# A two-layer diffusion / flow-matching step on one core: grid tokens by columns, norms in two halves, the last tiles of a stage in halves

## The reference

```python
def _modulate(x, mod, s, g):
    h = _rms_norm(x, g)
    return h * (1 + mod[:, :, 3 * s + 1]) + mod[:, :, 3 * s]
def _ffn_sublayer(x, mod, s, g, w13, w2):
    return x + 0.5 * mod[:, :, 3 * s + 2] * _swiglu(_modulate(x, mod, s, g), w13, w2)
```

## Time and profile before

| | |
|---|---|
| median of three runs | 3238.27 us |
| the profiled execution's own time | 3244.05 us |
| its span, first to last instruction | 3242.2 us |
| busy TensorE matmul / weight load | 3171.7 / 2917.7 us |
| busy VectorE / ScalarE / GpSimd | 1477.7 / 905.4 / 287.6 us |
| mean granted TensorE clock | 0.989 of full speed |
| moved by DMA | 300.25 MB, 93 GB/s |

### The profile page before, as it was taken

One profiled execution on the slowest core, in us unless ns is written; L12 is line 12 of the kernel. 1 busy time (PEld: TensorE's weight loads), 2 busy tenths in 40 slices (PEclk: granted clock), 3 DMA queues, 4 the chain that ended last, 5 costly groups with the idle time before them and its releaser, 6 DMA issues.

```text
span 3242.2 us, 48789 instructions
## 1 busy us (share of the span) xinstructions
PE 3171.7 (98%) x19680; PEld 2917.7 (90%) x19680; DVE 1477.7 (46%) x2313; ACT 905.4 (28%) x1279; POOL 287.6 (9%) x366
## 2 busy tenths in 40 slices
PE   8899999999999999999999999999999999999999
PEld 4899999976979999999999999868697876999999
DVE  3565634247654665624652525253443524422323
ACT  4122214234454312224212124222212222421222
POOL 1000001012001000001000001030301104000001
PEclk9999999989999999999999999999999999999999
DMA  8443422221101444422442222212121211122222
GB/s 210 151 170 132 156 78 65 86 70 25 61 1 53 149 163 136 162 82 75 160 152 75 102 69 84 84 59 72 65 72 65 79 68 36 65 78 78 72 72 72
DMA packets 84911, 300.25 MB, mean 93 GB/s; under 512 B 10399, under 2 KB 12735, under 8 KB 84000
## 3 DMA queue, kind: packets, MB, share of 16 engines
q1 hardware_dynamic: 57888, 206.77, 18.5%
q0 software_dynamic: 20704, 74.89, 8.1%
q10 hardware_dynamic: 6176, 16.54, 1.4%
HBM read 290.67 MB, written 8.44 MB: 92 GB/s over the span
## 4 chain that ended last, share of the span: by engine, by line
PE 90%; DVE 3%; ACT 2%; DMA 2%; issue 2%; POOL 1%; SPq 0%; ACTq 0%; DVEq 0%; POOLq 0%
PE ps L1227 36%; PE ps L1212 30%; PE ps L1366 11%; PE ps L1422 2%; PE ps L1588 2%; PE ps L1397 2%; PE ps L1597 2%; ACT tmp_g L507 1%; DMA ada<-in_ada 1%; PE ps L1410 1%; PE ps L1576 1%; DMA x<-in_xT 1%; PE ps L1243 1%; PE ps L1248 1%; DVE negmax L991 0%
## 5 line engine op out<-in xcount | busy, mean ns | idle before, releaser
L1227 PE MATMUL ps<-h,w 128*128 128x320 f32 x8640 | 1278.7, 310 | 19.1 <-DVE w L799 18.7
L1227 PEld LDWEIGHTS ps<-h,w 128*128 128x128 f32 x8640 | 1271.1, 188 | 25.1 <-DVE w L799 20.0
L1212 PE MATMUL ps<-g,w 128*128 128x320 f32 x5376 | 793.1, 309 | 1.5 <-DVE g L1173 1.5
L1212 PEld LDWEIGHTS ps<-g,w 128*128 128x128 f32 x5376 | 790.5, 188 | 2.2 <-issue 2.2
L799 DVE TENSOR_TENSOR w<-raw,w 128x1024 fp32r<-128x1024 f32 x383 | 460.8, 1224 | 288.6 <-ACT w L482 282.8
L482 ACT ACTIVATE w<-raw 128x1024 fp32r<-128x1024 f32 x207 | 216.3, 1060 | 562.6 <-PE ps L1212 457.9
L1366 PE MATMUL ps<-w,h 128*128 128x512 f32 x1596 | 368.5, 391 | 3.1 <-ACT rv L741 3.1
L1366 PEld LDWEIGHTS ps<-w,h 128*128 128x128 f32 x1596 | 298.0, 188 | 67.0 <-issue 4.7
L898 DVE TENSOR_TENSOR tmp_g<-tmp_s,ps 128x640 f32<-128x640 f32 x88 | 72.3, 821 | 598.3 <-ACT tmp_s L523 598.3
L819 DVE CUSTOM_DVE_ANT_0 prod<-ada,crow 128x1024 f32<-128x1024 f32 x256 | 298.5, 1219 | 17.5 <-DMA ada<-in_ada 17.4
L523 ACT ACTIVATE tmp_s<-ps 128x640 f32<-128x640 f32 x88 | 62.0, 705 | 846.2 <-PE ps L1227 846.2
(11 more groups left out here) (161 smaller groups left out, 1854.2 us busy)
## 6 DMA issues: line engine op xcount, KB each, us to landing
raw<-in_ws SPq DMA_DIRECT2D x383, 512.0 KB, 3.6
ada<-in_ada POOLq DMA_DIRECT2D x132, 512.0 KB, 3.9
ada<-in_ada ACTq DMA_DIRECT2D x6, 1024.0 KB, 16.9
rst<-in_state ACTq DMA_DIRECT2D x4, 1024.0 KB, 4.7
out_new_state<-rsx ACTq DMA_DIRECT2D x8, 512.0 KB, 2.7
bias<-rp_rep POOLq DMA_DIRECT2D x16, 224.0 KB, 4.3
x<-in_xT SPq DMA_DIRECT2D x1, 2560.0 KB, 25.6
crow<-in_crow POOLq DMA_DIRECT2D x1, 1024.0 KB, 6.0
```

The lines of the kernel that those rows point to most:

```text
L1212: mm = pe.matmul(pair_half(pr, half, width), w2[:, slot, wi, at:at + cols], rhs(k, ri)[:, half * width:(half + 1) * width], start=(k == 0 ...
L1227: mm = pe.matmul(pair_half(pr, half), w2[:, n % RING, wi, k * P:(k + 1) * P], h2[:, k, ri, half * HT:(half + 1) * HT], start=(k == 0 and w ...
```

## The change

**Tokens by grid columns.** The latents enter column by column (the host reorders them), and x goes back to grid rows in the first output projection of the attention (`add_by_rows`, which reads with a stride of 8 tokens); the query of the latent attention is reordered likewise (`latent_hi`, `latent_lo`, the rope). A block of 128 queries is then 16 grid columns, whose keys lie in a window of 192 or 256 latents (`NA_WINDOW`). Scores, maximum, exponential, normalisation run over 320 or 384 columns instead of 640, with 3 transposes and 3 value pieces in place of 5. V is made in 6 token tiles at window offsets (`V_AT`) in place of 5. The host lays out the bias rows, so `rp_rep` is gone; a head has one contiguous DMA of 128 KB and three GpSimd adds (640 columns in all). Two dummy matmuls of 512 columns (`dense`) stand in each unit, and the first score, the first exponential and the evacuation of V now overlap the V projection.

**Halves.** The last 4 tiles of an FFN (6 of the two projections ahead of norms 2 and 5) run twice: all for tokens 0 to 319, then all for 320 to 639. The first half's norm runs beside the second half's tiles; the broadcast, the sums and the h chunks are per half (16 half chunks in place of 8). The next stage's first two tiles are done by halves too. A chunk is now scale-and-multiply (VectorE), shift-and-split (ScalarE, one step instead of two), low part (VectorE). Weight splits of the next stage are moved ahead of or between the chunks, and `keep_warm` remains only at the start. The conditioning rows `crow` are loaded and passed through SiLU a second time before FFN 1, because the attention's buffers now cover them.

```diff
+MH = [5, 4, 2, 4, 4, 2, 4]
...
+            def half_lines(nn, h, l, s, after):
+                xn = x_cols if nn < 2 else x
+                dve.wait_ge(n_rb, 2 * nn + h + 1)
+                for k in range(KD + 2):
+                    if k < KD:
+                        if k >= 4:
+                            dve.wait_ge(h_lo, chunk(nn, h, k - 4))
+                        for c0, c1, st in half_parts(h):
+                            ins = dve.scalar_tensor_tensor(tmp_u[:, k % 4, c0:c1], xn[:, k, c0:c1], amul[:, k, st:st + 1],
+                                                           pair(2)[:, c0:c1], ALU.mult, ALU.mult)
+                        ins.then_inc(n_u, 1)
+                    if k >= 2:
+                        dve.wait_ge(h_hi, chunk(nn, h, k - 2))
+                        for c0, c1, st in half_parts(h):
+                            ins = dve.scalar_tensor_tensor(h2[:, k - 2, 1, c0:c1], tmp_u[:, (k - 2) % 4, c0:c1],
+                                                           mod[:, NMOD * l + 3 * s, k - 2, st:st + 1],
+                                                           h2[:, k - 2, 0, c0:c1].bitcast(fp32), ALU.add, ALU.subtract)
+                        ins.then_inc(h_lo, 1)
+                    if k in after:
+                        after[k]()
...
+            def norm_tail(nn, add1, lines, blocks):
+                add1(MH[nn])
+                if nn in PROJ:
+                    add1(MH[nn] + 1)
+                half_var(nn, 0)
+                if len(blocks) > 1:
+                    blocks[0]()
+                half_diag(nn, 0)
+                for m in range(MH[nn] + (2 if nn in PROJ else 1), KD - 2):
+                    add1(m)
+                lines(0, {1: blocks[1] if len(blocks) > 1 else lambda: None, 2: lambda: add1(KD - 2),
+                          3: lambda: add1(KD - 1), 6: lambda: half_var(nn, 1), 7: lambda: half_diag(nn, 1)})
+                lines(1, {3: blocks[-1]})
...
+                    for h in range(2):
+                        for m in range(mh, KD):
+                            n = rb + 2 * nf + m
+                            if h == 0:
+                                have(n)
+                            half_free(NORM_AFTER[q], xb + 8 * r, m, h)
+                            half_tile(n % RING, m % 3, of_g, h, nf).then_inc(wt_free if h else dn_half, 1)
+                            if h and m == mh:
+                                half_sum(NORM_AFTER[q], 0)
+                            elif h and m == mh + 1:
+                                half_rb(NORM_AFTER[q], 0)
...
+            def halves(ns, prs, nn):
+                for h in range(2):
+                    for k in range(KD):
+                        if nn and h == 0 and k == 4:
+                            half_sum(nn, 1)
+                        if nn and h == 0 and k == KD - 1:
+                            half_rb(nn, 1)
+                        pe.wait_ge(h_lo, chunk(nn, h, k))
+                        for n, pr in zip(ns, prs):
+                            for wi, ri in ((0, 0), (0, 1), (1, 0)):
+                                mm = pe.matmul(pair_half(pr, h), w2[:, n % RING, wi, k * P:(k + 1) * P],
...
 attend:
                 for g in range(g0, g1):
                     if g + 2 < g1:
                         score_mm(g + 2, na)
+                    if na:
+                        dense(1)
                     weight_mm(g, na)
+                    if na:
+                        dense(1)
                     if g - 1 >= g0:
                         value_mm(g - 1, na)
...
-            pool.dma_start(a["rp_rep"].rearrange("r (e w) -> r e w", w=RPW),
-                           a["rpb"].rearrange("r (o w) -> r o w", o=1).to_broadcast([NAH * RPR, RP_REP, RPW])
-                           ).then_inc(rp_rep, 16)
```

More of the change, by code:

```diff
@@ L526, in ffn @@
                                            tmp_g[:, u, :], ACT.Copy).then_inc(g_hi, 1)
-                    for m in range(KD):
+                    peel = int(r == 0 and q > 0)
+                    if peel:
+                        up(0, True)
+                    with act.Fori(peel, nf // 2) as i:
+                        up(i, False)
+                    for m in range(KD if r < 2 else KD - 2):
                         n = rb + 2 * nf + m
@@ L906, in ffn @@
                                 ada_rows(i + jl, 3 * u, min(3 * u + 3, KD))
+                    peel = int(r == 0 and q > 0)
+                    if peel:
+                        up(0, True)
+                    with dve.Fori(peel, nf // step) as i:
+                        up(i, False)
                     if r == 0:
@@ L1058, in _ @@
             o_part(3, 4)
[L1059 to L1065 removed]
+            last_projection(2, n0, n0 + 27, mod[:, 5], EM_X + 8, 0, 2)
             ffn(1, 0, 2)
[L1067 removed]
             ffn(2, 1, 0)
[L1069 removed]
             dve.wait_ge(r_ld, 48)
@@ new lines, in half_free, with half_tile @@
+            def half_free(nn, xb, m, h):
+                if h == 0 and m - 3 >= MH[nn]:
+                    pe.wait_ge(x_h0, X_H0[nn] + m - 3 - MH[nn] + 1)
+                elif m >= 3:
+                    pe.wait_ge(x_upd, xb + m - 2)
+            def half_tile(slot, pr, rhs, h, kts, base=0):
+                for k in range(kts):
+                    at = base + k * P
+                    for wi, ri in ((0, 0), (0, 1), (1, 0)):
+                        mm = pe.matmul(pair_half(pr, h), w2[:, slot, wi, at:at + P], half_of(rhs(k, ri), h),
+                                       start=(k == 0 and wi == 0 and ri == 0), stop=(k == kts - 1 and wi == 1))
+                return mm
@@ L1281, in ffn, with up @@
                     step = 2
-                    with pe.Fori(0, nf // step) as i:
-                        for u in range(step):
+                    def up(i, u0):
+                        for u in range(u0, step):
                             pe.wait_ge(up_free, i * step + (f0 + u + 1))
@@ L1318, in _ @@
             pe.wait_ge(const_ld, 144)
-            norm_sum(0)
+            for h in range(2):
+                half_sum(0, h)
             for j in range(2):
@@ L1419, in value_mm @@
                 r0 = 64 * (h % 2)
-                if b:
+                if b and na:
+                    for kt, (_, tile, k0, k1) in enumerate(NA_CHUNKS[b]):
+                        mm = pe.matmul(ps[r0:r0 + 64, 6, (b - 1) * P:b * P], va_na[tile][k0:k1, h * 64:h * 64 + 64],
+                                       pt[k0:k1, kt, (b - 1) * P:b * P], start=(kt == 0), stop=(kt == 2))
+                elif b:
                     for kt in range(5):
@@ L1761, in shape_constants, with bias_rows @@
     return c
+def bias_rows(rpb):
+    wide = np.pad(rpb, ((0, 0), (0, 0), (8, 8)))
+    out = np.empty((NAH, 16, ROWS, 32, ROWS), np.float32)
+    for c in range(16):
+        for r in range(ROWS):
+            out[:, c, r] = wide[:, NA_ROWS - 1 - r:2 * NA_ROWS - 1 - r, 15 - c:47 - c].transpose(0, 2, 1)
+    return out.reshape(NAH, P, NA_SPAN)
 def columns(v):
```

663 lines of the change are left out of this document (441 added, 222 removed).

## The result

The changed kernel takes 3200.31 us (median of 4 runs, 3195.97 to 3202.63). The kernel before took 3235.69 in the same comparison (4 runs, 3232.69 to 3241.33). The ratio is 0.9887, with a 95% interval of 0.9868 to 0.9906. So it is faster by 35 us where 67 had been forecast. 3200.31 lies 0.3 us outside the range of 3136 to 3200. The profiled execution took 3198.98 us (span 3197.3, before 3242.2), so 44.9 us of span have to be accounted for.

What follows compares the result with a forecast made beforehand. TensorE, holding 90% of the chain that ended last, was taken as the bound. Start 14, norms 27 and attention 28, less 2 for strides and clock, gave 67 us off 3244.05: 3177, or 3171 us at the median, range 3136 to 3200.

Steps and rivals of the forecast that it cites:

- The start: Kernel start: deleting the DMA that writes `rp_rep` ends TensorE's wait for the ada rows, saving 14 us, bounds 8 to 17.
- The 2 us charged for norm 0: Start: norm 0 grows because its squares become 5 whole and 6 half round trips; 2 us charged against 15.9 saved.
- The norms, in kind: Norms 1 to 5 and final: halves shorten stalls, with VectorE the limit; 34 us, 27 after collisions, bounds 5 to 40.
- The additions: Norms: GpSimd's additions of half-1 squares hold VectorE's low-part steps; 1.4 us for each of five norms, 7 taken off.
- The norms behind projections: Norms 2 and 5, six half tiles: lines start at 9.4 and end at 32.5; 8.2 and 7.0 us saved before collisions.
- Attention: Neighbourhood attention: narrower key windows bring a head from 15.0 to 11.2 us; 28 us saved, bounds 18 to 38.
- GpSimd's blocking: Neighbourhood attention: GpSimd's bias adds block the normalisation, so a head is taken at 11.2 us instead of 10.1.
- The rival that the chain alone paces the heads: Attention: the dependency chain, not TensorE, sets the pace; a head takes 13.5, 18 us more, 3189. Chance 0.13.
- The clock: Rival: thinner chunk stretches without keep_warm drop TensorE to half clock in attention and norms; 3283 us. Chance 0.04.
- Strides: Reads stepping 8 or 64 tokens (adds by rows, latent queries, rope): about equal price assumed, 1 us charged.
- The prediction's own upper case: Strided reads at doubled price: the rope, VectorE's longest work per latent projection, holds TensorE by up to 7 us.
- The median: The profiled execution before lies 5.8 us above the runs' median, so 3177 for it becomes a forecast of 3171.

Runs made afterwards that it cites:

- copy_late: The kernel before, with its replication of the bias table to DRAM issued behind norm 1 instead of at the start: 3231.72 us beside 3240.06, ratio 0.9973.
- split_late: The changed kernel, with the weight split at the fourth block of the two halved projections moved behind the first halves' squares and sum additions: 3182.46 us, ratio 0.9823.
- one_dummy: The changed kernel, with one idle matmul for each unit of neighbourhood attention instead of two, the one ahead of the transpositions kept: 3191.47 us, ratio 0.9856.
- no_dummies: The changed kernel without the 84 idle matmuls of neighbourhood attention, nothing else changed: 3233.27 us, ratio 0.9981.

## Why the prediction came out as it did

- **The start** was right: 15.7 measured, 14 forecast, and copy_late shows that it is the deleted transfer. The 2 us charged for norm 0 cannot be seen.
- **The norms, in kind.** That half chunks are VectorE's and that splits and blocking eat part of the gain held. The additions cost half of what was taken off, 3.6 for 7: two encounters a norm at three norms. Norms 1, 3, 4 and the final one gave 18.2, forecast 14.8. The surplus is norm 4's: the chain of before waits 3.40 us there for the load of the decay (`lgd`), of which the prediction kept 2.4, and the chain of after has no such wait.
- **The norms behind projections: this step failed.** "Norms 2 and 5 have six half tiles ... the add of tile 5 waits until 9.0, so lines start at 9.4": this took the first sum as ready when TensorE reached it. I had listed what stands behind the waiting split for the chunks, and not for the squares ahead of the sum, although the ring of four slots and six tiles in halves fix it on paper. The sum came 7.7 us late at both norms, and the wait with the slower matmuls behind it cost 14.6 us (split_late). With the split moved, the lines start at 9.5.
- **Attention** came out at 21 and not 28, and 6 of the 7 are the heads (96.9 us for the eight, where the sum had 90.7 with the drain). The mis-sized term is TensorE's own work in a head: 10.1 in the sum, 12.5 measured without idle time. An idle matmul is 0.34 us ahead of the transpositions and 0.23 behind, not 0.227, which makes 0.6 a head. The rest is real work in short groups, for which I had taken the pace of ten matmuls in a row: the three value pieces of a unit take 0.80 to 1.08 us, not 0.74. The 1.1 us a head for GpSimd's blocking, which brought the forecast to 11.2, can't be seen on TensorE. The rival that the chain alone paces the heads (13.5) fell, though the chain is close behind (one_dummy). V and what stands between it and the heads took 1 us more.
- **The clock** rival, given 0.04, did not come true, but only thanks to the idle matmuls. Without them a head costs 17.5 us. The prediction weighed heads at half clock without seeing how much hung on them.
- **Strides** I took at 1 "as every trace row of VectorE goes by columns alone": it was 5.5. The rows had no strided read, so they could not speak for equal price. The prediction's own upper case, a doubled price with the rotary work holding TensorE by up to 7, was nearer. The Trainium skill's rule ("SBUF — State Buffer", "Door 1: The DMA port swizzle") was right in direction; the page gives no factor for VectorE, and here the operation took 1.65 times as long.
- **The median.** I took off 5.8 us since the profiled execution of before lay above its median. The one of after lies 1.3 below its own, so the offset belonged to the run and not to the kernel. That is 7 of the 29 us between 3171 and 3200; the other 22 are span.

Added up, against the forecast of 67 of span: norms -12.7, attention -7.0, strides and clock -3.4, start +1.7, and 0.7 less in the feed-forwards and by rounding: 44.9.

## What to carry to other kernels

When a tile is cut in halves, go through each engine's queue and ask of every instruction ahead of the first half's work whether it needs the second half. One weight split that did cost 14.6 us at two norms whose halves were to gain 12.4. Before a gain of a few us is put down to an edit, compare the stages that the edit does not touch: here they differed by 1 to 2 us from one execution to the next, with the granted clock. Treat idle matmuls as instructions with a price and a yield: take them away and read the granted clock, then halve them. Of a price that no row shows, take the end that hurts when the operation lies on the path.

## What the hardware did that I had not expected

- A VectorE operation on 32 x 512 float32 whose second input steps by 32 bytes took 1.149 us, contiguous 0.696. From PSUM and SBUF at 128 x 512 it was 1.228 against 0.742.
- VectorE's low-part step of 192 columns (two inputs in SBUF) was held for 0.6 us when it met a GpSimd addition; the same kind of step with one input in PSUM was not.
- One idle matmul of 512 columns for each unit of attention was enough for a granted clock of 1.00. With none it was 0.50, although TensorE was shown busy all the time.
- The runs of the kernel before lie up to 14 us apart (3231.78 to 3245.35, 19 runs), and those of copy_late too (3223.55 to 3237.15, 10 runs). The 10 runs of no_dummies lie within 4.2, the 4 of the changed kernel within 6.7. The mean granted clock goes with the time (0.992 in the fastest run of the kernel before, 0.989 in the slowest). The first two alone read their bias through the replicated table. Whether that is the reason wasn't tried.
